# Expert retrieval on one core: tile 0's search, head by head, placed among tile 0's gathers

## The reference, cut to what matters

```python
q = (xc @ w_query).reshape(128, 8 heads, 2, 128)
s = einsum('thcd,hckd->thck', q, keys)             # 128 keys for each half
top_s, top_i = top_k(s, 16)
cand = top_s[:, :, 0, :, None] + top_s[:, :, 1, None, :]
best_s, best_j = top_k(cand, 16)                   # 16 experts a head
idx = (top_i0 * 128 + top_i1) at best_j            # of 16384 experts
gate = softmax(best_s)
act = gelu(einsum('thkd,td->thk', u_table[idx], xc))
y = einsum('thk,thkd->td', gate * act, v_table[idx])
```

## Time and profile before

| | us |
|---|---|
| median of 3 runs (lowest, highest) | 3525.19 (3522.11, 3529.10) |
| the profiled execution, its own time | 3523.02 |
| its span (first to last instruction) | 3521.2 |
| DVE busy | 2222.2 (63%) |
| PE busy | 2364.3 (67%) |
| ACT busy | 1010.7 (29%) |
| q0 (gathers): MB, share of 16 DMA engines | 1140.92, 79.8% |
| L1633, the products: busy, mean of one | 1325.0, 1226 ns |
| L1372, the gathers' issue: busy, mean of one | 1258.3, 1157 ns |

### The profile page before, as it was taken

How to read it: one execution, slowest core, us unless ns; L and a number is a source line. 1 busy time by engine, 2 the same in 40 slices (tenths; PEclk the granted TensorE clock), 3 DMA queues, 4 the chain that set the end, 5 groups by cost and what they waited for, 6 DMA issues and landing times.

```text
span 3521.2 us, 35625 instructions
## 1 busy us (share of the span) xinstructions
PE 2364.3 (67%) x9377; PEld 967.5 (27%) x9377; DVE 2222.2 (63%) x5008; ACT 1010.7 (29%) x3384; POOL 1322.6 (38%) x1229
## 2 busy tenths in 40 slices
PE   6997654476568566856685677567756765676676
PEld 3554434142114111411141124113311321241121
DVE  5344235557856775687568656855795578568754
ACT  2121211232333223233322332232233323332222
POOL 0010300344444444434444444444444434444442
PEclk9998777797688778967896778678867886897799
DMA  4111241699999999999999999999999999999998
GB/s 159 57 55 53 50 161 54 286 412 415 385 392 421 415 385 400 412 412 388 408 416 406 390 405 417 398 385 421 417 388 399 417 407 384 415 419 417 390 422 346
DMA packets 192652, 1212.96 MB, mean 344 GB/s; under 512 B 28952, under 2 KB 35416, under 8 KB 51688
## 3 DMA queue, kind: packets, MB, share of 16 engines
q0 software_dynamic: 156672, 1140.92, 79.8%
q1 hardware_dynamic: 35416, 69.28, 5.7%
q10 hardware_dynamic: 320, 0.07, 0.0%
HBM read 1194.51 MB, written 15.55 MB: 344 GB/s over the span
## 4 chain that ended last, share of the span: by engine, by line
DMA 29%; PE 22%; DVE 16%; issue 12%; ACT 5%; POOL 2%; DVEq 0%; SPq 0%; POOLq 0%; ACTq 0%; PEldq 0%
DMA uv_ring<-in_uv_table,idx 28%; PE ACC L1790 13%; PE TQ L1745 7%; DVE uv_ring L1633 5%; DVE S L1597 2%; DVE picks L1598 2%; DVE S L1596 2%; POOL uv_ring L1372 2%; ACT dg L1466 1%; ACT dot L1459 1%; PE OP L1726 1%; DMA wq<-in_w_query 1%; ACT dot L1449 1%; DVE dot L1633 0%; DVE pos L1528 0%
## 5 line engine op out<-in xcount | busy, mean ns | idle before, releaser
L1790 PE MATMUL ACC<-uv_ring,dg 128*64 128x512 f32 x4352 | 1472.8, 788 | 919.0 <-ACT dg L1466 918.3
L1372 POOL DMA_INDIRECT uv_ring<-in_uv_table,idx x1088 | 1258.3, 1157 | 1807.0 <-PE ACC L1790 1357.0
L1633 DVE CUSTOM_DVE_ANT_0 uv_ring<-uv_ring,xn 128x1024 f32<-128x1024 f32 x1088 | 1325.0, 1226 | 791.7 <-DMA uv_ring<-in_uv_table,idx 728.9
L1790 PEld LDWEIGHTS ACC<-uv_ring,dg 128*64 128x64 f32 x4352 | 343.7, 167 | 1930.8 <-ACT dg L1466 1396.9
L1449 ACT ACTIVATE dot<-dot 128x2 f32<-128x2 f32 x544 | 110.5, 203 | 1749.2 <-DVE dot L1633 1748.9
L1466 ACT ACTIVATE dg<-stack,dot 128x64 f32<-128x64 f32 x1088 | 327.8, 341 | 53.0
L1745 PEld LDWEIGHTS TQ<-glu_and_queries,wq 128*128 128x128 f32 x2304 | 266.4, 194 | 66.3 <-issue 64.7
L1745 PE MATMUL TQ<-glu_and_queries,wq 128*128 128x128 f32 x2304 | 280.5, 280 | 1.4 <-DMA wq<-in_w_query 1.2
L1459 ACT ACTIVATE dot<-gate,dot 128x1 f32<-128x1 f32 x1088 | 261.2, 287 | 17.7
L507 PE MATMUL PJ<-w_in,xT 128*128 128x512 f32 (+1 forms) x432 | 158.7, 528 | 1.5 <-DMA w_in<-in_w_in 1.5
L507 PEld LDWEIGHTS PJ<-w_in,xT 128*128 128x128 f32 x432 | 82.9, 192 | 79.2 <-issue 74.0
(11 more groups left out here) (319 smaller groups left out, 1653.2 us busy)
## 6 DMA issues: line engine op xcount, KB each, us to landing
uv_ring<-in_uv_table,idx POOLq DMA_INDIRECT x1088, 10.8
glu_and_queries<-in_w_glu SPq DMA_DIRECT2D x9, 1024.0 KB, 17.1
wq<-in_w_query SPq DMA_DIRECT2D x1, 8192.0 KB, 33.1
xt<-in_x SPq DMA_DIRECT2D x9, 512.0 KB, 3.4
xr<-scratch_x SPq DMA_DIRECT2D x9, 512.0 KB
w_in<-in_w_in SPq DMA_DIRECT2D x2, 2048.0 KB, 10.8
xk<-in_x SPq DMA_DIRECT2D x8, 512.0 KB, 3.2
scratch_x<-xk SPq DMA_DIRECT2D x8, 512.0 KB, 2.6
```

Of the source, the lines that this page charges most:

```text
L1372: pool.indirect_dma_start(out=ring[:, s_ % RING, :], out_offset=None, in_=a["uv_table"], in_offset=bass.IndirectOffsetOnAxis(ap=idx[:, s_: ...
L1633: V.tensor_tensor_reduce(row, row, xn[:, g, :], 1.0, 0.0, ALU.mult, ALU.add, dot[:, s_:s_ + 1]).then_inc(dots, 1)
L1790: ins = nc.tensor.matmul(ACC[GT * g:GT * (g + 1), b, :], dg[:, n % DG, :], ring[:, n % RING, D + 512 * b:D + 512 * b + 512], start=False, ...
```

## The change

1. *Tile 0's search goes head by head.* Ahead of the first turn only h = 0 to 2 of tile 0 and the turned rows are done; then queries and scores of all eight heads (PE and ACT), on DVE the whole search of head 0, and the first `best16` step of heads 1 to 3. The rest is cut into pieces A (best16 of both halves), B (candidates, their best16, the maximum), C and C2 (the match, in quarters of four places; C2 also turns the head's indices) and D (gates). They are placed by slot in a written-out "first" turn (turn 0). POOL waits for each head's indices at slots 0, 16, 32 and so on; ACT waits for each head's gates.
2. *Tile 1's preparation* runs wholly in the first turn: step s at slot s up to slot 51 (past the turned rows), then 1.15 steps a slot, so that it ends at slot 118.
3. The loop runs turns 1 to 6.
4. *No spreading of picks on PE any more.* DVE turns indices and gates out of SBUF itself, in one copy or product for each pair of halves; for the first 96 slots at step (7, 13), which is slot 109 of a steady turn, for the rest at slot 12 of the next.
5. w_query is laid out by head and loaded as eight DMAs of 1 MB, head 0's ahead of keys, place and spread; stack and g_fin come last.

```diff
+        def first_steps(s_):
+            lo, hi = 3 * KS + 3, NSLOT - 10
+            return s_ if s_ < lo else min(NSLOT, lo + (s_ - lo) * (NSLOT - lo) // (hi - lo))
...
+            if turn == "first":
+                own = [(1, i // KS, i % KS) for i in range(first_steps(s_), first_steps(s_ + 1))]
+                return own + ([(2, 0, j)] if h == EH - 1 else [])
...
+        BEST_AT = {1: 3, 2: 11, 3: 20, 4: 29, 5: 38, 6: 52, 7: 66}
+        FIRST_HEADS = {at + n: (e, piece) for e, at in BEST_AT.items() for n, piece in ((0, "B"), (2, "C"), (3, "C2"), (5, "D"))}
+        FIRST_HEADS |= {10: (4, "A"), 18: (5, "A"), 27: (6, "A"), 36: (7, "A")}
...
 POOL, retrieve
+                        if turn == "first" and s_ % KS == 0:
+                            pool.wait_ge(first["idx"], s_ // KS + 1)
...
 ACT, first_gates(e), at the slot of piece B
+                    act.wait_ge(first["nmax"], e + 1)
+                    A(ex[:, e, :], best[:, e, :], ACT.Exp, bias=nmax[:, e:e + 1],
+                      accum_out=esum[:, e:e + 1]).then_inc(first["ex"], 1)
...
 DVE
+                def take_gates(h0, h1, groups=GROUPS):
+                    for j in range(GROUPS):
+                        for g in range(groups):
+                            ...
+                            ins = V.tensor_tensor(units(gate, j, h0, h1, groups)[:, g], src,
+                                                  bcast(esum[rows, h0:h1], KS // GROUPS, 2), ALU.mult)
+                def first_head(e, piece):
+                    if piece == "A":
+                        dve.wait_ge(first["S"], e + 1)
+                        for n in range(2):
+                            best16(top_v[:, e, n, :], top_i[:, e, n, :], S[:, i + n, :])
+                    elif piece == "B":
+                        dch_(V.tensor_copy(top_f[:, head], top_i[:, head]))
+                        dch_(V.tensor_scalar(top_f[:, head, 0, :], top_f[:, head, 0, :], float(KEYS), None, ALU.mult))
+                        pairwise(top_v[:, head], first_cand, ALU.add)
+                        dch_(pairwise(top_f[:, head], first_cid, ALU.add), True)
+                        best16(best[:, e, :], pos[:, e, :], first_cand[:, 0, :])
+                        V.tensor_copy(pos_f[:, e, :], pos[:, e, :])
+                        dch_(V.tensor_scalar(nmax[:, head], best[:, e, 0:1], -1.0, None, ALU.mult))
+                    elif piece in ("C", "C2"):
+                        n = KS // 4
+                        for k0 in range(0, KS // 2, n) if piece == "C" else range(KS // 2, KS, n):
+                            dch_(V.tensor_tensor(quarter[:], bcast(place[:], n, 1), bcast(pos_f[:, e, k0:k0 + n], NCAND, 2), ALU.is_equal))
+                            dch_(V.tensor_tensor(quarter[:], quarter[:], first_cid[:].to_broadcast([P, n, NCAND]), ALU.mult))
+                            dch_(V.tensor_reduce(idx_f[:, e, k0:k0 + n], quarter[:], AX.X, ALU.add))
+                        if piece == "C2":
+                            take_picks(e, e + 1).then_inc(first["idx"], 1)
+                    else:
+                        dve.wait_ge(first["ex"], e + 1)
+                        dch_(V.reciprocal(esum[:, head], esum[:, head]))
+                        take_gates(e, e + 1).then_inc(first["gate"], 1)
...
 DVE, ahead of the first turn (h = 0 to 2 of tile 0 stay)
+                for piece in ("A", "B", "C", "C2"):
+                    first_head(0, piece)
+                for e in range(1, 4):
+                    first_head(e, "A")
+                first_head(0, "D")
+                for s_ in range(LEAD):
+                    product(0, s_)
+                retrieve("first", 0)
+                with dve.Fori(1, PT - 1) as t:
...
 PE
-                    elif at == (7, 14):
-                            ins = nc.tensor.matmul(spread_picks[:, g].rearrange("p v n -> p (v n)"), spread[:, g, :],
-                                                   picks[:].rearrange("p v h k -> p (v h k)"), start=True, stop=True)
+                for e in range(1, EH):
+                    first_queries(e)
+                    if e == 1:
+                        spread_rows(0, 0)
+                    first_scores(e)
+                pe.wait_ge(first["qT"], EH)
+                spread_rows(0, 1)
```

More of the change, by code:

```diff
@@ L1451, in weigh @@
                 def weigh(t, s_):
-                    if s_ == 0:
+                    if isinstance(t, int) and t == 0:
+                        if s_ % KS == 0:
+                            act.wait_ge(first["gate"], s_ // KS + 1)
+                    elif s_ == 0:
                         k["gate_ready"].of(act, t)
@@ L1482, in retrieve @@
                             diagonal(t, s_)
-                            if prep := prepared(turn, t, s_):
+                            if turn == "first" and FIRST_HEADS.get(s_, ("", ""))[1] == "B":
+                                first_gates(FIRST_HEADS[s_][0])
+                            for prep in prepared(turn, t, s_):
                                 prepare(*prep)
@@ L1614, in take_early @@
[L1614 to L1619 removed]
+                        if isinstance(t, int) and t == PT:
+                            k["gate_ready"].mark(take_gates(0, EH, 1))
+                            k["idx_ready"].mark(take_picks(0, EH, 1))
+                        else:
+                            k["gate_ready"].mark(take_gates(0, EARLY // KS))
+                            k["idx_ready"].mark(take_picks(0, EARLY // KS))
@@ L1653, in retrieve @@
                 def retrieve(turn, t):
-                    turn_now[0] = t
+                    turn_now[0] = None if turn == "first" else t
                     for s_ in range(LEAD, slots_of(turn)):
                         product(t, s_)
-                        if s_ == KS - 4 and turn != "samples":
+                        if s_ == KS - 4 and turn in ("steady", "eighth"):
                             take_rest(t)
-                        if s_ == TAKE and turn != "samples":
-                            take_early(t + 1)
-                        if prep := prepared(turn, t, s_):
+                        if turn == "first" and s_ in FIRST_HEADS:
+                            first_head(*FIRST_HEADS[s_])
+                        for prep in prepared(turn, t, s_):
                             prepare(*prep)
@@ L1675, in _ @@
                 dve.wait_ge(early, 48)
-                for h in range(EH):
+                for h in range(3):
                     for j in range(KS):
@@ L1884, in host_layout @@
         "ident": np.eye(P, dtype=np.float32), "stack": np.tile(np.eye(P // 2, dtype=np.float32), (2, 1)),
-        "spread": np.concatenate([np.tile(np.eye(P // 2, dtype=np.float32), (1, 2)) if r == g else np.zeros((P // 2, P), np.float32)
-                                  for r in range(2) for g in range(2)]).reshape(2, 2, P // 2, P).transpose(0, 2, 1, 3).reshape(P, 2 * P),
+        "spread": np.einsum("gh,ij,c->hjgci", np.eye(2), np.eye(P // 2), np.ones(2)).reshape(P, 2 * P).astype(np.float32),
         "minus_half": np.full((P, 1), -0.5, np.float32),
```

195 lines of the change are left out of this document (124 added, 71 removed).

## The result

The changed kernel takes 3478.14 us (median of 4 runs, 3472.99 to 3484.24); the kernel before takes 3525.18 on the same chip (4 runs, 3522.11 to 3529.10). The ratio is 0.9864, 95% interval 0.985 to 0.9879: faster by 47 us, and outside the range of 3420 to 3462. A second measurement of the same kernel (experiment 8) gave 3478.27 and 0.9869.

The account below looks back on a forecast made before the run. Retrieval was taken as bound by DMA pace, with DVE setting it at the match steps. From the profiled 3523 us: minus 88 (earlier gathers), minus 3 (loop restart), plus 7 (takes) gave 3439, forecast 3440, range 3420 to 3462.

Parts of the forecast that it names:

- First gather: Start of retrieval: head 0's indices ready at 555.1 instead of 641, so gathers begin 86.7 us earlier.
- 128 query matmuls in 16.26 us: PE before the first turn: 0.127 us per matmul, so head 0's 16 query matmuls take 2.0 us.
- product 1 isn't held long: Start of turn 0: ACT copies the last spread rows by 568.5, so slot 1's product hardly waits.
- Some four rows are ahead in the ring: Turn 0, slots 48-63: rows fetched ahead leave twelve to come at 2.48 us, so the eighth takes 30.
- the prediction's own 15 us: Ring in turn 0: a row needs about 15 us, 3.6 from product end to gather and 10.8 to land.
- 3 us for DVE's waits on PE and ACT: First turn: 3 us added for waits without slack, putting turn 1's product 0 at 897 instead of 894.
- DVE's work: First turn in eighths of 16 slots: DVE's terms of work, 322.2 us within a sum of 326.
- ACT's exps hidden: First turn: exp and table loads, some 3.1 us per head, delay ring rows by 3 us but stay hidden.
- Takes, +7: Slot 109 of seven steady turns: gate products and casts on DVE add 1.3 us each, taken as +7.
- The branch, -3: Loop from turn 1: one restart fewer gains 0 to 4.7 us, taken as 3; unrolling itself costs nothing.
- the second (3471, turn 0 355): First turn: DVE over budget by 13 us of prices and 15 to 20 of waits; 3471 us, chance 0.14.
- The third, gathers that stop between heads: First turn: POOL waits for each next head's indices, 21 us a head, 148 in all; 3588 us, chance 0.03.

Follow-up runs that it names:

- experiment 8: Changed kernel once more, unchanged, as a base on another measurement: 3478.27 us, ratio 0.9869.
- Experiment 1: Changed kernel with the second group's rows of x spread right behind head 2's queries, into another PSUM buffer: 3474.23 us, ratio 0.9852.
- experiment 11: Changed kernel with pieces re-placed, early row spread, whole matches, 100 empty ACT instructions, and PE's queries one head ahead of the scores: 3460.06 us, ratio 0.9819.
- Experiment 2: Changed kernel without the matches of heads 1 to 7 in turn 0, about 36 us less DVE work: 3461.51 us, ratio 0.9817.
- experiment 4: Changed kernel with turn 0's gathers from slot 8 on fetching half a table row (4 KB instead of 8): 3481.49 us in one execution.
- experiment 6: Changed kernel with search pieces and tile 1's steps moved so that light eighths get more work: 3478.12 us, ratio 0.9857.
- experiment 5: Changed kernel with ACT's exp of heads 1 to 7 replaced by identity, avoiding table loads: 3481.51 us in one execution.
- experiment 3: Kernel before with only DVE taking indices and gates from SBUF, without PE's spreading of the picks: 3528.15 us against 3523.76, ratio 1.0011.
- experiment 12: Kernel before with only turn 0 written out and the loop from 1: 3528.76 us against 3524.03, ratio 1.0019.

## Why the prediction was wrong

The direction was right, and so was where the gain comes from, the earlier first gather; the size was not: 3440 against 3478.14. Against the profiled execution (3472.99) 34 us are missing, and they lie in turn 0: two steps of its sum failed.

- *First gather:* 84 earlier, predicted 86.7. The pieces cost what was said: B of a head 3.36 (583.34 to 586.70; predicted 3.4), twelve quarters 5.4 (5.5), picks 0.71 and 0.86 (0.6), D 0.9 (0.8). But head 0's queries and copies took 5.5 + 0.4 and not 2.6, hidden in part by an upstream that ran some 2 us early.
- *128 query matmuls in 16.26 us, "so 0.127 each", and 16 of them a head:* the first failed step. The row held only half of the queries; a second row of 128 stands behind it in the trace of before (557.06, 14.53 us). One head is 32 PE instructions, 3.74 us. The price of one instruction was near (0.117), the count was not. PE's eight heads end at 576, the second group's rows x are copied at 579.75 and not by 568.5, "product 1 isn't held long" became 8.6 us, and the ring stood still until 585.80. Worth 9 in the first eighth. Experiment 1 took DVE's wait away and got 4 of it back, experiment 11 shortened the stretch behind it and got another 4.
- *"Some four rows are ahead in the ring":* the second failed step, and the largest: 20 us in the two light eighths. The ring has eight places, but the prediction's own 15 us from the end of a product to the landing of the next row are six of them, and places come free in pairs. It used this number to show that ACT's 3 us are hidden, and not to ask what credit is left. The 15 was itself partly luck: the gather at 666.04, read as 3.6 us behind the product that ended at 662.4, is the one for slot 11 and waited for slot 3; the place of that product (slot 5) went to the gather at 668.52, 6.1 behind. And the gathers of turn 0 land after 8.8 us (median), not 10.8. Experiment 2 shows that less DVE work mostly turns into waiting for rows, experiment 4 that this waiting is about one third the pace of the DMA, experiment 6 that evening out the eighths gives 8.3 back.
- *3 us for DVE's waits on PE and ACT:* 5.4 for ACT's scores alone (2.94 at 757.87, and 2.44 at 802.25), most of the 6.6 by which the eighth at 64 is over.
- *DVE's work:* 326.8 against 322.2, so 4.6 of the excess are prices and small gaps.
- *ACT's exps hidden:* about 3.5 of turn 0 (experiment 5, one execution).
- *Takes, +7:* not settled. The match eighth has the +1.5, and the next one gives 1.3 back, which would make it near nothing; in the kernel after, turns 1 to 7 take 2362.5, before 2363.9. But the time of the takes alone is +4.4 (experiment 3), near the +5 that the term stands for, and the scatter between traces is as large as the term.
- *The branch, -3:* turn 1's first eighth took 43.6 instead of 46.9, as said. That a written-out turn costs nothing elsewhere is not so in the kernel before (experiment 12); in the changed kernel the last four slots of a turn aren't longer (10.2 against 10.3), so the loss isn't there.

Of the rivals the second (3471, turn 0 355) came nearest in time, but only in part by its mechanism: of its 13 us of prices 4.6 came, and its waits were to be small ones at every step. The waits that came stand in three places, 8.6 at the start, 22.3 for rows in two light eighths and 5.4 for ACT's scores. The third, gathers that stop between heads, had no part: POOL waited 0.3 us in all for indices after the first.

## What to carry to other kernels

When work is moved beside a stream of transfers, don't compare sums over the whole stretch: take it in pieces no longer than the buffer's credit, which is the number of buffers less the round trip from release to landing in steps of the pace. Here that is 8 less 6; no run here has another number of buffers. A light piece can't pay for a heavy one beyond that. And before a price per instruction is multiplied, check the count of a row against the program: it may be a part of the work, and one matmul of the program may be several instructions.

## What had not been expected of the hardware

A 128x128 float32 matmul of the program stands in these traces as two PE instructions of 0.117 us (32 in 3.74). The first 32 took 5.54: the granted clock was 0.65 between 535.0 and 541.5, after PE had been busy for 2.0 of the 7.8 us before, and 1.00 from 553 to 576. On one chip ACT was idle for 5 to 8.4 us in each of four traces while the first gathers ran, 2 to 5 of it with its input ready; six traces from two other chips have no such stop. Two executions of one kernel differed by 5.5 us ahead of the first gather with the same instructions, so a trace's own upstream has to be taken off before a start is compared. And a restart of a loop that is taken away (5.7 us of stops less) can leave the kernel slower, here by 4.7 us.
